# Expert rows scaled by their gates and added to one row per token by the scatter, with combine, final norm and the next norm in one stage

## What is computed

```python
# h: (512, 1024), after norm and modulation
scores = sigmoid(h @ w_router)                        # 64 experts, 8 groups
# best 4 groups, then best 6 experts of them, per token
gate = scores[chosen] / scores[chosen].sum() * 2.5
for each token t, each of its 6 experts e:
    routed[t] += gate * (silu(h[t] @ w_gate[e]) * (h[t] @ w_up[e])) @ w_down[e]
shared = (silu(h @ w_sh_gate) * (h @ w_sh_up)) @ w_sh_down
x = x + gate_f * (shared + routed)                    # gate_f: one row of 1024
x = rms_norm(x, g_final)                              # end of block 1
h3 = rms_norm(x, norm_mix_2)                          # first step of block 2
```

## Time and profile before

| | us |
|---|---|
| median of 3 runs | 2176.08 (2175.59 to 2190.18) |
| profiled execution | 2178.05 |
| its span in the trace | 2176.0 |
| TensorE busy | 1871.6 |
| VectorE busy | 1317.6 |
| ScalarE busy | 1013.0 |
| GpSimd busy | 679.6 |

### The profile page before, as it was taken

How to read it: one execution, slowest core, us unless ns; L and a number is a source line. 1 busy time by engine, 2 the same in 40 slices (tenths; PEclk the granted TensorE clock), 3 DMA queues, 4 the chain that set the end, 5 groups by cost and what they waited for, 6 DMA issues and landing times. The chain is left out here.

```text
span 2176.0 us, 28527 instructions
## 1 busy us (share of the span) xinstructions
PE 1871.6 (86%) x8582; PEld 1455.7 (67%) x8582; DVE 1317.6 (61%) x1608; ACT 1013.0 (47%) x1304; POOL 679.6 (31%) x534
## 2 busy tenths in 40 slices
PE   5787999996839999999999950589989877998999
PEld 2664677775727888888888840456656556887887
DVE  1582564455758999999999937365466654333232
ACT  1321444432107888888888830354455533222221
POOL 0597891000053666666666620011101100000000
PEclk9798999998679999999999975799999988999999
DMA  6644642223029999999999936323210003332222
GB/s 250 164 155 144 173 141 62 64 68 122 21 81 362 362 374 360 368 372 370 374 362 357 358 106 241 92 73 78 50 44 30 20 10 117 97 96 77 97 96 78
DMA packets 168406, 373.52 MB, mean 172 GB/s; under 512 B 40588, under 2 KB 77992, under 8 KB 159880
## 3 DMA queue, kind: packets, MB, share of 16 engines
q1 hardware_dynamic: 148888, 325.45, 43.7%
q0 software_dynamic: 19440, 47.05, 6.6%
HBM read 355.77 MB, written 29.29 MB: 177 GB/s over the span
## 5 line engine op out<-in xcount | busy, mean ns | idle before, releaser
L108 DVE TENSOR_TENSOR exp_parts<-exp_raw,exp_parts 128x2048 fp32r<-128x2048 f32 x192 | 435.0, 2291 | 56.4 <-ACT exp_parts L1768 56.0
L1768 ACT CAST exp_parts<-exp_raw 128x2048 fp32r<-128x2048 f32 x192 | 365.1, 1915 | 79.6 <-DMA exp_raw<-in_w_exp_up 66.6
L102 PE MATMUL ps<-exp_parts,xgT 128*128 128x512 f32 x1536 | 377.3, 401 | 6.6 <-issue 6.4
L102 PEld LDWEIGHTS ps<-exp_parts,xgT 128*128 128x128 f32 x1536 | 285.8, 189 | 77.6 <-issue 12.0
L102 PE MATMUL ps<-exp_parts,exp_hT 128*128 128x512 f32 x768 | 196.3, 405 | 2.1 <-DVE exp_hT L108 2.1
L102 PE MATMUL ps<-h4T,w_up_parts 128*128 128x512 f32 x768 | 176.1, 392 | 8.5 <-DVE w_up_parts L108 8.5
L1661 POOL DMA_INDIRECT xg<-h_rows,row_index x64 | 148.5, 2321 | 110.4 <-issue 108.6
L102 PE MATMUL ps<-w_down_parts,hidden_parts 128*128 128x512 f32 x768 | 176.4, 392 | 7.1 <-DVE w_down_parts L108 7.1
L102 PEld LDWEIGHTS ps<-h4T,w_up_parts 128*128 128x128 f32 x768 | 145.1, 189 | 39.3 <-ACT w_up_parts L144 8.7
L102 PEld LDWEIGHTS ps<-w_down_parts,hidden_parts 128*128 128x128 f32 x768 | 145.5, 190 | 37.9 <-issue 7.5
L102 PE MATMUL ps<-h3T,w_parts 128*128 128x512 f32 (+1 forms) x576 | 158.4, 430 | 12.9 <-DVE w_parts L108 12.9
(11 more groups left out here) (417 smaller groups left out, 3222.9 us busy)
## 6 DMA issues: line engine op xcount, KB each, us to landing
exp_raw<-in_w_exp_gate SPq DMA_DIRECT2D x130, 512.0 KB, 5.9
exp_raw<-in_w_exp_up SPq DMA_DIRECT2D x130, 512.0 KB, 7.8
exp_raw<-in_w_exp_down SPq DMA_DIRECT2D x64, 1024.0 KB, 7.9
w_up_raw<-in_w_up SPq DMA_DIRECT2D x15, 1024.0 KB, 5.2
w_down_raw<-in_w_down SPq DMA_DIRECT2D x15, 1024.0 KB, 5.1
yk<-y_rows SPq DMA_DIRECT2D x8, 1536.0 KB, 16.9
w_raw<-in_w_in SPq DMA_DIRECT2D x42, 256.0 KB, 3.3
modw<-in_w_mod SPq DMA_DIRECT2D x4, 2048.0 KB, 24.0
```

The lines of the kernel that those rows point to most:

```text
L102: mm = nc.tensor.matmul(out, left[a], right[b], start=start and i == 0, stop=stop and i == 2)
L108: return nc.vector.tensor_tensor(dst, x, high.bitcast(F32), ALU.subtract)
L1768: nc.scalar.copy(dst, src).then_inc(s_hi[kind], 1)
```

## The change

The scatter adds. Each pair's record in `row_assignments` is now a number and its gate, two floats. ScalarE scales the expert's result by the gate of its row (`row_gate`) as it copies it, and GpSimd's scatter (L1688 after) adds the rows to `moe_rows`, which has one row per token and 128 spare rows; pad places add to a spare row each (`row_out`). Two scatters may meet in a token, so a scatter waits until the one before has landed. `moe_rows` starts as the shared expert's result, which ScalarE copies from PSUM to `h` and SyncE stores before the experts. So the gates are worked out ahead of the counts, where two casts of shared weights stood; these come behind the destinations. The combine stage loads one row per token, and does `gate_f`, the sum, the final norm, the norm mix2, its transposes and parts in one pipeline over four tiles.

```diff
@@ -1267,9 +1271,13 @@
             sp.wait_ge(s_bes, 32)
             sp.dma_start(r["be_row"][:], r["be_dram"].rearrange("b a -> a b")).then_inc(s_bes, 16)
             sp.wait_ge(s_scat, 16 * NT * TOPK)
-            sp.dma_start(rb[:], r["row_asg"].rearrange("(b p) a -> b (p a)", p=P)).then_inc(s_rb, 16)
+            sp.dma_start(rb[:], r["row_asg"].rearrange("(b p) a -> b p a", p=P)).then_inc(s_rb, 16)
+            for t in range(NT):
+                sp.wait_ge(s_dc, 2 * t + 2)
+                sp.dma_start(r["acc"][t * P:t * P + P, :], h[:, t, :]).then_inc(s_dst, 16)
             sp.wait_ge(s_bes, 48)
-            sp.wait_ge(s_hst, 16 * NT)
+            sp.wait_ge(s_gf, 16)
+            sp.wait_ge(s_dst, 16 * NT)
...
@@ -1280,7 +1288,7 @@
                 for k in range(TOPK):
                     pool.indirect_dma_start(
                         r["row_asg"], bass.IndirectOffsetOnAxis(ap=r["dest"][:, t, k:k + 1], axis=0),
-                        asg[:, t, k:k + 1], None).then_inc(s_scat, 16)
+                        asg[:, t, k, :], None).then_inc(s_scat, 16)
...
+            pe.wait_ge(s_dc, 1)
+            pe.wait_ge(s_rb, 16)
+            for a in range(2):
+                tr = nc.tensor.transpose(g.ps[:, DOWN_BANK[0], a * NB:a * NB + NB], rb[:, :, a], g.ident[0:NB, 0:NB])
+            tr.then_inc(s_rbt, 1)
...
+            act.wait_ge(s_hst, 16 * NT)
+            for c in range(8):
+                act.wait_ge(s_dn, c + 1)
+                n = c % 2 * 512
+                nc.scalar.copy(h[:, c // 2, n:n + 512], g.ps[:, DOWN_BANK[c], :]).then_inc(s_dc, 1)
...
             v.memset(cnt[:, 4, :], 1.0).then_inc(s_A, 1)
-            shared_low(1)
-            shared_low(2)
+            v.tensor_copy(asg[:, :, :, 0], ids[:])
+            for t in range(NT):
+                link(v.tensor_tensor(tmp[:], oh[:, t], sc[:, t, :].unsqueeze(1).broadcast_to([P, TOPK, E]), ALU.mult))
+                link(v.tensor_reduce(gate[:, t, :], tmp[:], AX.X, ALU.add))
+                link(v.tensor_reduce(gsum[:, 0, t:t + 1], gate[:, t, :], AX.X, ALU.add))
+                link(v.reciprocal(gsum[:, 1, t:t + 1], gsum[:, 0, t:t + 1]))
+                link(v.tensor_scalar(asg[:, t, :, 1], gate[:, t, :], gsum[:, 1, t:t + 1], ROUTED_SCALE, ALU.mult, ALU.mult))
...
             v.tensor_copy(r["be_col"][:], be[:, E:E + 1]).then_inc(s_be, 1)
+            shared_low(1)
+            shared_low(2)
...
             dve.wait_ge(s_rbt, 1)
+            v.tensor_copy(r["row_gate"][:], g.ps[:, DOWN_BANK[0], NB:2 * NB])
             link(v.tensor_copy(lists[:], g.ps[:, DOWN_BANK[0], 0:NB]))
             v.tensor_copy(r["row_asg_cols"][:], lists[:])
             link(v.tensor_scalar(r["row_tok"][:], lists[:], S - 1, None, ALU.bitwise_and))
-            link(v.tensor_scalar(lists[:], lists[:], float(TOPK * S), 4096.0, ALU.is_ge, ALU.mult))
+            link(v.tensor_scalar(pads[:], lists[:], P - 1, None, ALU.bitwise_and))
+            link(v.tensor_scalar(pads[:], pads[:], float(S), None, ALU.add))
+            link(v.tensor_tensor(pads[:], pads[:], r["row_tok"][:], ALU.subtract))
+            link(v.tensor_scalar(lists[:], lists[:], float(TOPK * S), None, ALU.is_ge))
+            link(v.tensor_tensor(pads[:], pads[:], lists[:], ALU.mult))
+            link(v.tensor_tensor(r["row_out"][:], r["row_tok"][:], pads[:], ALU.add))
+            link(v.tensor_scalar(lists[:], lists[:], 4096.0, None, ALU.mult))
             v.tensor_tensor(r["row_tok"][:], r["row_tok"][:], lists[:], ALU.add)
...
-            def scatter(b, u):
+            def scatter(b, u, i):
                 pool.wait_ge(s_y, b - 3)
-                nc.gpsimd.tensor_copy(oidx[:, u % 2:u % 2 + 1], r["row_asg_cols"][:, bass.ds(b - 4, 1)]).then_inc(s_oi, 1)
+                nc.gpsimd.tensor_copy(oidx[:, u % 2:u % 2 + 1], r["row_out"][:, bass.ds(b - 4, 1)]).then_inc(s_oi, 1)
                 pool.wait_ge(s_oi, b - 3)
+                if u:
+                    pool.wait_ge(s_st, 64 * i + 16 * u - 64)
+                else:
+                    pool.sem_inc(s_seen, 1)
+                    with pool.If(i > 1):
+                        pool.wait_ge(s_st, 64 * i - 64)
+                        pool.sem_inc(s_seen, 1)
                 pool.sem_inc(s_seen, 1)
                 for n in rows_to_move(b - 4):
-                    pool.indirect_dma_start(r["y"], bass.IndirectOffsetOnAxis(ap=oidx[0:n, u % 2:u % 2 + 1], axis=0),
-                                            y[0:n, u % 2, :], None, bounds_check=TOPK * S - 1,
-                                            oob_is_err=False).then_inc(s_st[u % 2], 16)
+                    pool.indirect_dma_start(r["acc"], bass.IndirectOffsetOnAxis(ap=oidx[0:n, u % 2:u % 2 + 1], axis=0),
+                                            y[0:n, u % 2, :], None, bounds_check=S + P - 1,
+                                            compute_op=ALU.add).then_inc(s_st, 16)
...
                 if not (first and u < 3):
-                    act.wait_ge(s_st[o], 32 * i + 16 * ((u - 3) // 2) + 16)
-                nc.scalar.copy(y[:, o, :], g.ps[:, 5:7, :].rearrange("p b n -> p (b n)")).then_inc(s_y, 1)
+                    act.wait_ge(s_st, 64 * i + 16 * (u - 2))
+                nc.scalar.activation(y[:, o, :], g.ps[:, 5:7, :].rearrange("p b n -> p (b n)"), ACT.Copy,
+                                     scale=r["row_gate"][:, bass.ds(b - 1, 1)]).then_inc(s_y, 1)
...
-def combine_stage(g, r, gate_f, gain):
...
         def _(sp):
+            sp.dma_start(gf[:], bcast_rows(gate_f, D)).then_inc(s_gf, 16)
             for t in range(NT):
-                if t >= 3:
-                    sp.wait_ge(s_used, TOPK * (t - 2))
-                for h in range(2):
-                    sp.dma_start(yk[:, t % 3, 3 * h:3 * h + 3, :], rows[:, t, 3 * h:3 * h + 3, :]).then_inc(s_y[t % 3][h], 16)
+                sp.dma_start(rows[:, t, :], acc[t * P:t * P + P, :]).then_inc(s_rows[t], 16)
                 if t == 0:
-                    sp.dma_start(gain_sb[:], bcast_rows(gain, D)).then_inc(s_gain, 16)
+                    sp.dma_start(gain[:], bcast_rows(io["g_final"].rearrange("(a d) -> a d", a=1), D)).then_inc(s_gain[0], 16)
+                if t == 1:
+                    sp.dma_start(gain2[:], bcast_rows(io["norm_mix_2"], D)).then_inc(s_gain[1], 16)
...
+            for s in range(NT + 2):
+                if s < NT:
+                    square(0, s)
+                if 0 <= s - 1 < NT:
+                    root(1, s - 1)
+                if s < NT:
+                    root(0, s)
+                if 0 <= s - 1 < NT:
+                    high(s - 1)
+                if s < NT:
+                    square(1, s)
...
+            def add_rows(t):
+                if t == 0:
+                    dve.wait_ge(s_gf, 16)
+                dve.wait_ge(s_rows[t], 16)
+                link(v.tensor_tensor(rows[:, t, :], rows[:, t, :], gf[:], ALU.mult))
+                v.tensor_tensor(g.x[:, t, :], g.x[:, t, :], rows[:, t, :], ALU.add).then_inc(s_x, 1)
+            def mean(i, t):
+                dve.wait_ge(s_sq[i], t + 1)
+                v.tensor_scalar(stat[:, i, 1, t:t + 1], stat[:, i, 0, t:t + 1], 1.0 / D, EPS, ALU.mult, ALU.add).then_inc(s_ms[i], 1)
...
+            for s in range(NT + 2):
+                if s < NT:
+                    add_rows(s)
+                if 0 <= s - 1 < NT:
+                    mean(1, s - 1)
+                if 0 <= s - 2 < NT:
+                    low(s - 2)
+                if s < NT:
+                    mean(0, s)
+                if 0 <= s - 1 < NT:
+                    normed(1, s - 1)
+                if s < NT:
+                    normed(0, s)
...
+def moe(g, io, acc, gate_f):
     with ExitStack() as a:
-        r = {"row_asg": g.dram("row_assignments", [(BLOCKS + 4) * P, 1], I32), "be_dram": g.dram("be_d", [BLOCKS + 4, 1], I32),
+        r = {"row_asg": g.dram("row_assignments", [(BLOCKS + 4) * P, 2]), "be_dram": g.dram("be_d", [BLOCKS + 4, 1], I32),
              "n_dram": g.dram("n_d", [1, 1], I32), "h": g.dram("h2_rows", [S, D]),
-             "y": g.dram("y_rows", [TOPK * S, D]),
+             "acc": acc, "gate_f": gate_f,
              "be_row": g.sb("be_row", [1, BLOCKS + 4], I32, ctx=a), "be_col": g.sb("be_col", [P, 1], I32, ctx=a),
-             "n_col": g.sb("n_col", [P, 1], I32, ctx=a), "gate": g.sb("gate6", [P, NT, TOPK], ctx=a),
```

More of the change, by code:

```diff
@@ L1208, in ffn_front_stage @@
         be = g.sb("block_expert", [P, E + 2], ctx=st)
-        asg = g.sb("assignment_ids", [P, NT, TOPK], I32, ctx=st)
+        ids = g.sb("assignment_ids", [P, NT, TOPK], ctx=st)
+        asg = g.sb("assignments", [P, NT, TOPK, 2], ctx=st)
+        gate = g.sb("gate6", [P, NT, TOPK], ctx=st)
+        pads = g.sb("pad_pieces", [P, NB], I32, ctx=st)
         lists = g.sb("row_lists", [P, NB], I32, ctx=st)
-        rb = g.sb("row_blocks", [NB, P], I32, ctx=st)
-        rbf = g.sb("row_blocks_f", [NB, P], ctx=st)
+        rb = g.sb("row_blocks", [NB, P, 2], ctx=st)
         gain = g.mod[:, 0:D]
```

(15 more changed lines are left out.)

150 lines of the change are left out of this document (67 added, 83 removed).

## The result

The kernel after takes 2197.34 us (median), 1.0095 times the one before, 95% interval 1.0061 to 1.0129. So it is about 1% slower; 2204 was forecast. Measured again on a second chip it took 2203.33 us, 1.0101 [1.0067, 1.0135].

What follows compares the result with a forecast made beforehand. TensorE was taken to bound the expert stage, DMA engines close behind. 2178.05 + 4.6 (front) - 30.9 (combine and norm) + 52 (expert stage) = 2204 us, 1.3% over the median; range 2150 to 2285, the forecast case's own 2167 to 2236.

Steps and rivals of the forecast that it cites:

- Expert stage, the pace: Expert stage: landing plus 1.6 us per block, periods 10.2 us (blocks of 64) and 12.8 (of 128); +52 us.
- the three cases: Expert stage, the add's second read: free, 0.18 us a row, or 0.32 like the first; 0, 15 or 52 us, third taken.
- Expert stage, the way to TensorE: Expert stage: GpSimd's wait delays the next block's gather, and TensorE's transposes wait for that; the path of the +52 us.
- the 10 us of slack: Expert stage: the lag can grow some 10 us in all before TensorE waits, so 62 us of lateness cost 52.
- Expert stage, the size of a landing: Expert stage: 0.32 us per row and engine for each read, landings 8.6 us on small blocks, 11.2 on large.
- No cheap mending: Expert stage: the wait between adding scatters cannot simply be left out, so the chain's cost has no cheap mending.
- Front stage: Before the experts: gate work delays scatters by 1.2 us, and stores behind the list load come late; +4.6 us (1 to 8).
- Combine and norm: Combine stage and the norm after it: 38.2 us against 69.3, four tiles of 6.9 us; -30.9 us (-24 to -34).
- the rival: Combine stage: ScalarE and VectorE ping-pong at 9.5 us a tile, merged stage saves only 20 us; 2215 us, chance 0.05.
- The chain hidden: Expert stage: landing up to 8.15 us for a block of 64, so no added time; 2152 us, chance 0.27.
- Slow add: Expert stage: the add itself is slow, landings 9.9 and 13.7 us, 151 us more; 2303 us, chance 0.10.
- The DMA engines as bound: Expert stage: DMA traffic of 254.3 MB sets the pace, at 385 GB/s 36 us late; 2188 us, chance 0.10.

Runs made afterwards that it cites:

- the first execution: First profiled execution of the kernel after, 2191.1 us, the shortest of its four; its counts came 9 us early.
- apart: Kernel after with the norm mix2, its transposes and parts moved out of the combine stage into their own norm stage: 2203.54 us, 1.0101 times the kernel before.
- both plain scatters: Kernel before with each scatter waiting for the one before, 2177.59 us (stage 670.7); kernel after writing rows instead of adding, 2160.86 us (stage 674.5).
- the kernel before with the wait: Kernel before with only this added: each plain scatter waits until the one before has landed; 2177.59 us, 1.0001 times the kernel before.
- the one with early stores: Kernel after with the four stores of the shared expert's result issued ahead of the block list's load: 2204.48 us, 1.0113 times the kernel before.

## Why the prediction came out right, step by step

- *The end point.* 2178.05 + 4.6 - 30.9 + 52 gave 2204; the two medians are 2197.3 and 2203.3. The three terms measured +7.2, -28.4 and +46.6. Each has the right sign and is off by 2.5 to 5.4 us.
- *Expert stage, the pace.* Right: landing plus a fixed time of GpSimd per block, GpSimd waiting ahead of its scatter, the stage's pace. The fixed time was 1.8 us, not 1.6. The landing on small blocks was 8.4 (8.6 forecast), so their period is 10.2, as forecast; on the 13 large ones 10.15 (11.2 forecast), so 11.9 instead of 12.8. Of the three cases the one taken was the nearest.
- *Expert stage, the way to TensorE.* Wrong: "Behind GpSimd's new wait stands the gather of the next block, and TensorE's transposes wait for that". TensorE waited for the gather 1.2 us in all from 700 to 1240 us. ScalarE's copy to `y` waited for the scatter that had its buffer, 55.9 us in 45 waits. So the 10 us of slack, which were reckoned for the gather, had no ground: 59 periods grew by 48 us together, and 45 to 47 of them reached the stage. The forecast is near by luck in this: 62 us of longer periods were too many by 14, and 10 us were taken off that didn't come off.
- *Expert stage, the size of a landing.* In part wrong. The slope of 0.32 us for a row and engine was taken from two landings of the kernel before, and used twice, once for the write and once for the second read. From small to large blocks it gives 2.6 us more; 1.75 were measured. The fit above has 0.24 us for an adding scatter's row in all, read and write together, and 0.6 for the larger scatter. What the sum lacks is the issue: an adding scatter holds GpSimd 1.43 us at the least where a writing one needs 0.91, and up to 3.5 beside VectorE's casts, and the landing moves with that. An add lands 1.7 us later than a plain write on small blocks (8.40 against 6.73, a mean over 25 scatters of the kernel before), 1.5 with the same rows left out (8.22), and 2.1 on large ones (10.15 against 8.06, over 5). A row price too high stood for this missing term, which is luck.
- *Rule on the add in the DMA path.* The Trainium skill (Collectives: The Full Stack, "The bandwidth ceiling: the fold count and why AG ≠ RS ≠ AR") has two source reads and half the rate, for collectives. The engine time of 0.34 us for a scattered row against 0.18 agrees; the landing, 1.25 times as long, doesn't follow it.
- *"No cheap mending".* Refuted: two sets of rows keep the order that an add needs and take the wait out, for 6 us of combining and 33 to 35 us less in the stage.
- *Front stage.* +7.2 for +4.6. Up to SyncE's load of the list it was 2.8 instead of 1.2: VectorE's gate work put GpSimd's scatters back by 0.9, about as forecast, but the 24 scatters took 2.0 us more (2.4 in the first execution, 1073 ns each instead of 972). So "I leave GpSimd's price for one as it is" failed: two of them, of 2.1 and 1.9 us, stand beside VectorE's casts of shared weights, which the change had moved there. Behind that load it was 4.4 instead of 3.4: the late stores were on the path, for 1.7 to 2.2 us, and the rest falls to the operations on the list, by subtraction only.
- *Combine and norm.* -28.4 for -30.9: a tile took 6.6 us, forecast 6.9, but head and tail were 15 us instead of the 10.5 of the sum (0.8 of it behind VectorE's last operation). That merging is what shortens the stage, as the rival priced it, is refuted: apart it takes 39.3.
- *The rivals.* The chain hidden is what both plain scatters show (670.7 and 674.5), but the add's 1.7 us is just what keeps it from being hidden. Slow add: refuted by landings of 8.4 and 10.2 us where it has 9.9 and 13.7. The DMA engines as bound: not in the kernel after, whose casts don't wait for weights between 700 and 1240 us; once the chain is away they wait at times, but the stage doesn't follow it. That TensorE's clock would fall didn't come true: 0.99.

## What to carry to other kernels

An adding scatter that must wait for the one before makes a chain: landing plus the issuer's own time per block. Put that sum beside the pace of the bounding engine first: 8.6 us under 9.76 was free, 10.6 over it cost 45 us, and two targets in turn broke the chain for 6 us of combining. And when stages are joined at the same time as their work shrinks, price the two apart: here all the gain was in the smaller work.

## What the runs showed of the hardware

- An indirect DMA that adds to DRAM lands later than one that writes: 3.6 to 4.1 against 2.6 us for 33 rows with the DMA all but idle, 8.2 against 6.7 under load (mean of small blocks, empty rows left out in both). It holds the DMA engines 0.34 against 0.18 us for a row of 4 KB, and GpSimd at least 1.43 us against 0.91.
- Rows left out by bounds save little of the landing: with the DMA idle 3.7, 4.0 and 4.6 us for 20, 33 and 56 real rows out of 64 named, 4.6 to 4.8 with all 64 moved.
- GpSimd's issue of an adding scatter took, in the kernel after, 1.44 to 1.60 us when it started beside VectorE's operations that read PSUM, and 1.62 to 3.46 beside its subtractions of two SBUF tensors; the landing grew by one to two times the difference. VectorE's own operation stayed at 2.29 us.
- The router's stretch (540 to 550 us) ran at a granted clock of 0.50 in eleven executions and of 0.70, 0.89 and 0.91 in three, of kernels whose TensorE work is alike up to there. The counts come at 584 to 592 us in the eleven and at 577 to 581 in the three (the kernel before with the wait has 580.88, the one with early stores 577.03), and all that follows moves with them. A profile's span should be split at such a place before two kernels are compared by it.
